# A ring of weight chunks in a mixture-of-experts loop: low parts written in place, eight slots instead of six, four high buffers instead of three

## The reference, cut to what matters

```python
def expert_block(args):
    tok, e = args
    xb = hf[tok]
    gu = xb @ w_gate_up[e] + b_gate_up[e]        # 1024 x 2048 per expert
    gate, up = jnp.split(gu, 2, axis=-1)
    gate = jnp.minimum(gate, SWIGLU_LIMIT)
    up = jnp.clip(up, -SWIGLU_LIMIT, SWIGLU_LIMIT)
    act = (up + 1.0) * gate * jax.nn.sigmoid(SWIGLU_ALPHA * gate)
    return act @ w_down[e] + b_down[e]           # 1024 x 1024 per expert
```

## Time and profile before

| | |
|---|---|
| median of 3 runs | 1774.97 us (1774.8 to 1775.13) |
| the profiled execution's own time | 1766.66 us |
| its span, first to last instruction | 1764.9 us |
| PE busy | 1698.8 us, 96% |
| DVE busy | 1381.7 us, 78% |
| ACT busy | 1200.8 us, 68% |
| POOL busy | 713.1 us, 40% |
| DMA moved | 504.64 MB, 286 GB/s over the span |

### The profile page before, as it was taken

How to read it: one execution, slowest core, us unless ns; L and a number is a source line. 1 busy time by engine, 2 the same in 40 slices (tenths; PEclk the granted TensorE clock), 3 DMA queues, 4 the chain that set the end, 5 groups by cost and what they waited for, 6 DMA issues and landing times.

```text
span 1764.9 us, 24895 instructions
## 1 busy us (share of the span) xinstructions
PE 1698.8 (96%) x8477; PEld 1346.8 (76%) x8477; DVE 1381.7 (78%) x1048; ACT 1200.8 (68%) x967; POOL 713.1 (40%) x344
## 2 busy tenths in 40 slices
PE   6999999999999999999999999999999999999998
PEld 5878889777888987767767767767767767767776
DVE  4666776755334389999999999999999999999984
ACT  5565555433223368788788788788788788788775
POOL 6124233550000072355465365365365365365110
PEclk9999999999999999999999999999999999999999
DMA  5443343433336469999999999999999999999951
GB/s 177 122 129 85 121 122 107 121 108 119 96 96 231 164 218 397 391 404 392 399 402 392 399 401 392 402 406 388 404 404 391 405 400 398 402 400 395 408 201 49
DMA packets 150865, 504.64 MB, mean 286 GB/s; under 512 B 12733, under 2 KB 73285, under 8 KB 117173
## 3 DMA queue, kind: packets, MB, share of 16 engines
q1 hardware_dynamic: 141652, 478.49, 70.0%
q0 software_dynamic: 9104, 25.28, 6.0%
q10 hardware_dynamic: 48, 0.07, 0.0%
HBM read 487.63 MB, written 20.28 MB: 288 GB/s over the span
## 4 chain that ended last, share of the span: by engine, by line
PE 68%; DVE 14%; issue 9%; ACT 6%; POOL 2%; DVEq 0%; ACTq 0%; POOLq 0%
PE gu_ps L2395 13%; DVE split_l L1928 9%; PE gu_ps L2147 8%; PE gu_ps L2149 8%; PE gu_ps L2148 8%; PE dn_ps L2453 7%; PE gu_ps L2399 7%; PE dn_ps L2459 3%; ACT split_h L1303 3%; PE gu_ps L2409 2%; PE dn_ps L2652 1%; PE gu_ps L2652 1%; PE et_ps L2381 1%; DVE up_sb L1915 1%; PE gu_ps L2169 1%
## 5 line engine op out<-in xcount | busy, mean ns | idle before, releaser
L1928 DVE TENSOR_TENSOR split_l<-ring,split_h 128x2048 fp32r<-128x2048 f32 x384 | 864.8, 2285 | 71.0 <-ACT split_h L1303 69.3
L1303 ACT ACTIVATE split_h<-ring 128x2048 fp32r<-128x2048 f32 x384 | 729.9, 1913 | 113.8 <-PE gu_ps L2399 62.7
L914 POOL COPY icur<-slots 96x1 int32 x30 | 282.8, 9428 | 412.3 <-PE et_ps L2381 410.1
L1536 DVE TENSOR_TENSOR w_lo<-w_raw,w_hi 128x2048 fp32r<-128x2048 f32 (+1 forms) x45 | 104.3, 2318 | 128.8 <-ACT w_hi L1035 122.6
L2409 PE MATMUL gu_ps<-split_l,xgT_h 128*128 128x512 f32 x480 | 139.6, 412 | 17.8 <-DVE split_l L1928 14.0
L2147 PE MATMUL gu_ps<-hT_h,w_hi 128*128 128x512 f32 x392 | 154.6, 394 | 0.6 <-DVE acc L1589 0.6
L2149 PE MATMUL gu_ps<-hT_h,w_lo 128*128 128x512 f32 x392 | 152.7, 390 | 0.0
L2148 PE MATMUL gu_ps<-hT_l,w_hi 128*128 128x512 f32 x392 | 152.6, 389 | 0.0
L2395 PE MATMUL gu_ps<-split_h,xgT_h 128*128 128x512 f32 x512 | 140.6, 396 | 0.9 <-DVE xgT_l L1934 0.9
L2399 PE MATMUL gu_ps<-split_l,xgT_h 128*128 128x512 f32 x512 | 137.2, 390 | 0.0
L2395 PE MATMUL gu_ps<-split_h,xgT_l 128*128 128x512 f32 x512 | 137.2, 390 | 0.0
(11 more groups left out here) (426 smaller groups left out, 3242.1 us busy)
## 6 DMA issues: line engine op xcount, KB each, us to landing
ring<-in_w_gate_up SPq DMA_DIRECT2D x256, 1024.0 KB, 8.0
ring<-in_w_down SPq DMA_DIRECT2D x128, 1024.0 KB, 9.2
w_raw<-in_w_in SPq DMA_DIRECT2D x28, 1024.0 KB, 5.9
arow<-acum_rows POOLq DMA_DIRECT2D x16, 512.0 KB, 6.5
w_raw<-in_w_ssd_out SPq DMA_DIRECT2D x8, 1024.0 KB, 5.4
w_raw<-in_w_in SPq DMA_DIRECT2D x9, 512.0 KB, 6.1
w_raw<-in_w_mix_out SPq DMA_DIRECT2D x4, 1024.0 KB, 7.9
wpg<-in_w_ple_gate SPq DMA_DIRECT2D x2, 2048.0 KB, 19.9
```

What stands on the lines that cost most here:

```text
L914: g.tensor_copy(icur[:, :], col).then_inc(idx_done, 1)
L1303: a.activation(split_h[s % SPLIT][:, :], ring[s % RING][:, :], ACT.Copy).then_inc(hi_done, 1)
L1536: v.tensor_tensor(w_lo[RAW_SLOT[n]][:, 0:size], w_raw[RAW_SLOT[n]][:, 0:size], w_hi[HI_SLOT[n]][:, 0:size].bitcast(F32), ALU.subtract).the ...
L1928: v.tensor_tensor(split_l[s % SPLIT][:, :], ring[s % RING][:, :], split_h[s % SPLIT][:, :].bitcast(F32), ALU.subtract).then_inc(lo_done, 1)
```

## The change

Low parts are written over the raw chunk in the ring slot (`ring_low` is the same memory as `ring`, in the fast matmul type), `split_l` goes, and its 24 KB become the fourth `split_h` and ring slots 6 and 7. A load now waits until PE has used the chunk eight before it. `high` waits for the chunk four before it. 12 chunks an expert are no multiple of 8 slots, so loops run over pairs of experts (24 chunks). In the seams, `gate` and `halves_out` now come behind `high` 10, `half_gate` behind `high` 11, `turned_high` and `turned_low` behind chunk 12 and chunk 16, `half_down_out` behind `high` 14, `half_y_out` and `y_out` behind `high` 15. The first loads of slots 6 and 7 wait for nothing. The diff, cut to its core (the same renaming of slots in the five matmul functions is left out):

```diff
-RING = 6
-SPLIT = 3
+RING = 8
+FIRST = 6
+SPLIT = 4
...
-        ring = [here(f"ring{i}", [P, 2 * DM], F32) for i in range(RING)]
+        ring_off = top[0]
+        ring = [here(f"ring{i}", [P, 2 * DM], F32) for i in range(FIRST)]
+        top[0] = ring_off
+        ring_low = [here(f"ring_low{i}", [P, 2 * DM], F32R) for i in range(FIRST)]
...
         split_h = [here(f"split_h{i}", [P, 2 * DM], F32R) for i in range(SPLIT)]
-        split_l = [here(f"split_l{i}", [P, 2 * DM], F32R) for i in range(SPLIT)]
+        ring_off = top[0]
+        ring += [here(f"ring{i}", [P, 2 * DM], F32) for i in range(FIRST, RING)]
+        top[0] = ring_off
+        ring_low += [here(f"ring_low{i}", [P, 2 * DM], F32R) for i in range(FIRST, RING)]
...
         def chunk_at(j, e, i):
-            return j * NE * CHUNKS + e * CHUNKS + UP + i
+            pair, off = in_pair(e)
+            return j * NE * CHUNKS + pair * (2 * CHUNKS) + off * CHUNKS + UP + i
+
+        def slot_of(e, i):
+            return (in_pair(e)[1] * CHUNKS + UP + i) % RING
...
             def gate_up(j, e, i, of, k, first=False):
-                slot = (UP + i) % RING
+                slot = slot_of(e, i)
                 if not first:
-                    sp.wait_ge(lo_done, chunk_at(j, e, i) + 1)
+                    sp.wait_ge(chunk_used, chunk_at(j, e, i) + CHUNKS - RING + 1)
...
-            for k in range(RING, UP):
-                gate_up(0, 0, k - UP, 0, k)
+            for k in range(FIRST, UP):
+                gate_up(0, 0, k - UP, 0, k, True)
...
             def high(j, e, i):
                 at, s = chunk_at(j, e, i), UP + i
-                act.wait_ge(e_loaded[s % RING], raw_loaded(j, e, i))
+                act.wait_ge(e_loaded[slot_of(e, i)], raw_loaded(j, e, i))
                 act.wait_ge(chunk_used, at + CHUNKS - SPLIT + 1)
...
                 def rest(e, more, rows_in, rows_act, folds=None):
-                    turned_high(t0 + 3 + e * 2, xgT_h, rows_in, 1.0 if more else 1.0 / ALPHA)
-                    for i in range(12, 14):
-                        high(j, e, i)
+                    n = number(e)
+                    high(j, e, 12)
+                    turned_high(t0 + 3 + n * 2, xgT_h, rows_in, 1.0 if more else 1.0 / ALPHA)
+                    high(j, e, 13)
+                    high(j, e, 14)
                     if folds is not None:
-                        half_down_out(e, e)
-                    high(j, e, 14)
+                        half_down_out(e, n)
+                    high(j, e, 15)
                     if folds is None:
-                        y_out(j, e, 11, n0 + e)
+                        y_out(j, e, 11, n0 + n)
                     else:
-                        half_y_out(e, folds)
-                    high(j, e, 15)
+                        half_y_out(n, folds)
                     if more:
-                        turned_high(t0 + 4 + e * 2, actT_h, rows_act, 1.0 / ALPHA)
-                        for i in range(16, 22):
+                        high(j, e, 16)
+                        turned_high(t0 + 4 + n * 2, actT_h, rows_act, 1.0 / ALPHA)
+                        for i in range(17, 22):
                             high(j, e, i)
 
                 def expert(e, more, rows_in=ROWS, folds=None):
-                    gate(j, e, UP - 1, n0 + e + 1)
                     high(j, e, 10)
+                    gate(j, e, UP - 1, n0 + number(e) + 1)
                     high(j, e, 11)
...
                 def half_expert(e, folds):
-                    halves_out(e, e + 1)
                     high(j, e, 10)
+                    halves_out(e, number(e) + 1)
+                    high(j, e, 11)
                     half_gate(folds)
-                    high(j, e, 11)
...
             def low(j, e, i):
                 dve.wait_ge(hi_done, at + 1)
-                v.tensor_tensor(split_l[s % SPLIT][:, :], ring[s % RING][:, :], split_h[s % SPLIT][:, :].bitcast(F32),
-                                ALU.subtract).then_inc(lo_done, 1)
+                v.tensor_tensor(ring_low[slot_of(e, i)][:, :], ring[slot_of(e, i)][:, :],
+                                split_h[s % SPLIT][:, :].bitcast(F32), ALU.subtract).then_inc(lo_done, 1)
...
                 def expert(e, more, half_next=False):
-                    up(ROWS, chunk_used, chunk_at(j, e, UP - 1) + CHUNKS + 1, n0 + e + 1)
                     low(j, e, 10)
+                    up(ROWS, chunk_used, chunk_at(j, e, UP - 1) + CHUNKS + 1, n0 + number(e) + 1)
                     low(j, e, 11)
```

More of the change, by code:

```diff
@@ L520, in program @@
         pen_done, last_idx = sem("pen_done"), sem("last_idx")
-        e_loaded = [sem(f"e_loaded{i}") for i in range(RING)]
+        e_loaded = [sem(f"e_loaded{i}") for i in range(FIRST)] + yT_loaded[0:RING - FIRST]
         hi_done, lo_done, et_hi = sem("hi_done"), sem("lo_done"), sem("et_hi")
@@ L729, in weights, with expert_loads @@
                     sp.wait_ge(order_done, 1)
-                with sp.Fori(1 if ahead else 0, NE - 1) as e:
-                    of, after = (position(sp, e), position(sp, e + 1)) if ahead else (e, e + 1)
-                    bias_parts(j * NE + e + 1, after)
+                def expert_loads(e):
+                    n = number(e)
+                    of, after = (position(sp, n), position(sp, n + 1)) if ahead else (n, n + 1)
+                    bias_parts(j * NE + n + 1, after)
                     for k in range(UP):
@@ L736, in weights @@
                         down(j, e, UP + r, of, r)
+                with sp.Fori(0, PAIRS) as i:
+                    for off in (1, 2) if ahead else (0, 1):
+                        expert_loads((i, off))
+                if not ahead:
+                    expert_loads(NE - 2)
                 of = position(sp, NE - 1) if ahead else NE - 1
@@ L748, in weights @@
                 alone(sp)
-            for k in range(RING):
+            for k in range(FIRST):
                 gate_up(0, 0, k - UP, 0, k, True)
@@ L1300, in high @@
                 at, s = chunk_at(j, e, i), UP + i
[L1301 removed]
+                act.wait_ge(e_loaded[slot_of(e, i)], raw_loaded(j, e, i))
                 act.wait_ge(chunk_used, at + CHUNKS - SPLIT + 1)
[L1303 removed]
+                a.activation(split_h[s % SPLIT][:, :], ring[slot_of(e, i)][:, :], ACT.Copy).then_inc(hi_done, 1)
             def gate(j, e, i, n):
@@ L1425, in one_pass @@
                     with act.Fori(0, PAIRS - 1) as i:
-                        expert(i * 2 + 2, True, HALF, i * 2 + 2)
-                        half_expert(i * 2 + 3, i * 2 + 3)
+                        expert((i, 2), True, HALF, i * 2 + 2)
+                        half_expert((i, 3), i * 2 + 3)
                     expert(NE - 2, False, folds=NE - 2)
                 else:
-                    with act.Fori(0, NE - 2) as e:
-                        expert(e, True)
+                    with act.Fori(0, PAIRS) as i:
+                        expert((i, 0), True)
+                        expert((i, 1), True)
                     expert(NE - 2, False)
@@ L2012, in one_pass @@
                     with dve.Fori(0, PAIRS - 1) as i:
-                        expert(i * 2 + 2, True, True)
-                        half_expert(i * 2 + 3, i * 2 + 3)
-                else:
-                    with dve.Fori(0, NE - 2) as e:
-                        expert(e, True)
+                        expert((i, 2), True, True)
+                        half_expert((i, 3), i * 2 + 3)
+                else:
+                    with dve.Fori(0, PAIRS) as i:
+                        expert((i, 0), True)
+                        expert((i, 1), True)
                 expert(NE - 2, False)
@@ L2403, in half_gate_up @@
             def half_gate_up(e, i, k):
-                at, s = chunk_at(0, e, i), (UP + i) % SPLIT
-                for part, ready, count in ((split_h, hi_done, at + 1), (split_l, lo_done, at + RING + 1)):
+                at, high_part, low_part = chunk_at(0, e, i), split_h[(UP + i) % SPLIT], ring_low[slot_of(e, i)]
+                for part, ready, count in ((high_part, hi_done, at + 1), (low_part, lo_done, at + RING + 1)):
                     pe.wait_ge(ready, count)
                     for b in range(4):
-                        o = t.matmul(gu_ps[:, b * 512:b * 512 + 512], xgT_h[:, k, :], part[s][:, b * 512:b * 512 + 512],
+                        o = t.matmul(gu_ps[:, b * 512:b * 512 + 512], xgT_h[:, k, :], part[:, b * 512:b * 512 + 512],
                                      start=False, stop=False)
@@ L2423, in half_down @@
             def half_down(e, r):
-                at, s = chunk_at(0, e, UP + r), (2 * UP + r) % SPLIT
-                for part, ready, count in ((split_h, hi_done, at + 1), (split_l, lo_done, at + RING + 1)):
+                at, high_part, low_part = chunk_at(0, e, UP + r), split_h[(2 * UP + r) % SPLIT], ring_low[slot_of(e, UP + r)]
+                for part, ready, count in ((high_part, hi_done, at + 1), (low_part, lo_done, at + RING + 1)):
```

(4 more changed lines are left out.)

75 lines of the change are left out of this document (42 added, 33 removed).

## The result

The changed kernel takes 1858.24 us (median of 4 runs, 1854.7 to 1860.93) where the kernel before took 1775.05 beside it: a ratio of 1.0467 (95% interval 1.0451 to 1.0484), 83 us slower. The forecast was 1759 with a range to 1785. It failed in its sign; the third rival named this place and 1859 us. The profiled execution is that of 1860.93 us, its span 1859.2.

The account below looks back on a forecast made before the run. Three high buffers were taken to bind, loads next at 64.8 us a pair: 15 x 1.0 + 0.8 = 15.8 us off 1775.0 gives 1759 us, range 1741 to 1785 (forecast's own range 1747 to 1770).

Parts of the forecast that it names:

- What bounds before: Expert loop: three high buffers limit DVE's lead, so PE waits 5.3 us a pair for low parts at half chunks.
- Part 1: Four high buffers: one chunk more lead cuts PE's wait from 5.3 to 2.6 us, the pair from 65.8 to 63.1.
- Part 2: Loads of a pair: bounds 63.2 on average and 65.8 us, 64.8 taken; loads late next, gain 1.0 us a pair.
- Part 3: Ring of eight slots released by PE: taken as 0, bounds -0.5 to +0.9 us a pair.
- Part 4: Low parts written in place by DVE: same instruction and size, taken as 0, at most 0.4 us a pair.
- Part 5: Seams, start and end: reordered instructions and start 0, the stretch behind the last pair -0.8 us.
- rival 3: POOL gets no turn in DVE's longer runs, so the index copy and gather come late: up to 1859 us; chance 0.20.
- end case: Worst case of rival 3: index copy 16.8 us later, PE loses up to 8.7 us a pair, 84 us net, 1859 us.
- the rule: Shared port pair held for one instruction's length: POOL's copy would wait some 2.2 us, the change cost nothing.
- Rival 1: The lead counts in full: gathers cost the ring less, pair 63.1 us, gain 40 us, 1735 us; chance 0.13.
- Rival 2: DMA engines full already: gain at most 0.3 us a pair, 1770 to 1775 us; chance 0.22.

Follow-up runs that it names:

- e9: Kernel before the change with each w_down load halved (a sixth of the loads' bytes less), engine work as before: 1774.83 us, ratio 0.9997.
- e10: e5 with each w_down load halved, engine work as before: 1745.3 us, ratio 0.9832 to the kernel before.
- e13: e5 with POOL's copies of the scatter's index and the next weight moved ahead of the wait for the transposes: ratio 1.0058 to the kernel before.
- e5: Changed kernel, with DVE waiting in the seam ahead of a half stretch until POOL's index copy is done: 1774.3 us, ratio 1.0041 to the kernel before.
- e1: Changed kernel without the fourth high buffer and with the old seams; in-place low parts and eight slots kept: 1771.97 us, ratio 1.0029 to the kernel before.
- e2: Changed kernel with POOL's index copy moved ahead of its wait for the transposes: 1780.95 us, ratio 1.0074 to the kernel before.
- e12: Kernel before the change with POOL's index copy moved ahead of its wait for the transposes: 1778.35 us, ratio 1.0014.
- e15: e2 with the scatter's index and next weight copied early too, and DVE waiting until the gather is issued: ratio 1.0116 to the kernel before.
- e14: e2 with the scatter's index and next weight copied early too, no pause of DVE: ratio 1.0048 to the kernel before.
- e11: Changed kernel with each w_down load halved, engine work and index copy as they were: 1841.69 us, ratio 1.0371 to the kernel before.
- e6: Changed kernel with each low part made by two DVE subtractions of half the size: 1883.46 us, ratio 1.0664 to the kernel before.
- e8: e2 with halves_out back ahead of high 10 and DVE pausing until the gather is issued: 1781.47 us, ratio 1.0082 to the kernel before.

## Why the prediction was wrong

**What bounds before.** Right. The three buffers did, not the loads: e9 has a sixth fewer bytes and the same 65.8 us.

**Part 1.** Right in mechanism and nearly in size. PEld's waits for low parts fell from 5.3 to 1.4 us a pair, further than the 2.6 forecast, and with loads and POOL out of the way a pair takes 63.6 us (e10), where 63.1 was worked out.

**Part 2.** The order was right (the loads are late next), the size wrong. The pair with whole loads is 66.0 to 66.2 us (e13, e5), not 64.8. I took a value below the upper bound of 65.8 although the queues' shares summed to 101%; the upper bound itself was too low. The gain of 1.0 us a pair was none. That is 15 us of the miss of 99.

**Part 3.** Taken as 0. In the pairs that holds (e1, 65.8 us); behind the last pair all kernels with eight slots lose 5 us, by a stall of ACT that nothing in the traces explains. The bounds did not cover an end of the program.

**Part 4.** Right: the subtraction takes 2285 ns in place, in 384 instructions, as in the row of before at 2.29.

**Part 5 and the sum.** Here the forecast failed. The sum had no term for POOL; its whole lateness stood in rival 3, at 0.20 and "most of it near the small end". In place of nothing it was 6.6 us of wait of PE and 2.2 of lower clock in the pair shown; less what the lead gained that is 5.9 us a pair, 82 in all. The rival's chain of reasons was right: DVE's runs without a pause keep POOL out, the change makes them longer, and PE's slack of 4.8 to 8.1 us is used up (7.0 us of the delay went into it). Its end case gave 8.7 us of wait and 84 us, against 8.8 of wait and clock together and 83 us. That the totals meet so closely is partly luck: the end case delayed the copy by 16.8 us, where copy and issue together came 13.6 us later, and it had neither the clock nor the 5 us at the end. Two things made me hold the rival for small. I asked how much later the copy would end, and it was only 2.2 us longer (12.54 against 10.32). That the issue behind it would meet the next run of subtractions, 14.05 us instead of 2.70, was not asked, though the earlier trace rows had a sign of it: the issue starts at 1028.20, just behind the gap in which the copy ended and inside a subtraction, and ends at 1030.90. And "if loads bind, DVE must pause somewhere" let one term hide the other: the loads would have bound at 66, but by then PE had already stopped for the rows, and the loads never got late.

I let the rule weigh against the row as well. The Trainium skill, SBUF — State Buffer, section SBUF: two separate sides, has the loser of the shared port pair wait for one whole instruction. The traces here go against that as a bound: POOL waited through runs of four, six and twelve. The same section warns of DMAs issued by GpSimd, whose descriptors can't be written while VectorE runs an instruction in a two-port mode. The 14.05 us look like such a wait, and I had not read it onto this gather. The section Who interferes with whom excludes tensor_tensor from the effect on descriptors, by inference, and has it contend with GpSimd's reads. In the changed kernel, e2, e5 and e12 the issue takes 9 to 14 us beside little but tensor_tensor; whether it waits to read its indices or to write its descriptors no run here tells.

**Rivals.** Rival 1 (1735) is what e10 comes near with light loads. Rival 2 (nothing gained, 1770 to 1775) is what is left when POOL's lateness is repaired: 1.0041 in e5, 7 us, of which the stall at the end is some 5. Rival 3 is what happened.

A version that beats the kernel before with whole loads was not found. The fourth buffer with its seams buys nothing as long as the loads need 66 us a pair.

## What to carry to other kernels

When a change makes VectorE run without gaps, list every instruction of GpSimd that overlaps such a run, the issues of indirect DMAs as well as the copies, and price each at the whole run rather than at one instruction. Add the times in series, then compare them with the slack of the engine that needs the result. If they don't fit, a semaphore wait of VectorE where GpSimd has to act can be cheap: in e5 one took 76 us back. A wait for the longer step isn't sure to be: e15 lost 13 us against e14, for a cause that is open. And before widening a buffer, run the old kernel and the new with fewer bytes loaded, to see which of them the loads hold. A larger wait can hide the answer: e11 still stood at 1841.69 us, and only e10, with POOL's lateness repaired, showed the loads.

## What the runs showed of the hardware

- GpSimd's copy of 96 numbers takes 0.18 us at the least (in the changed kernel) and up to 27.51 us (e6) beside VectorE subtractions with both inputs in SBUF; the issue of an indirect DMA 1.0 us and up to 15.8 (e8). Idle gaps of VectorE of 0.19 to 0.44 us were enough to let it in (the copy of dcur in e5 ends at 1046.09, in the one of 0.19 us; the index copy of the kernel before in the one of 0.44); more boundaries without gaps were not (e6).
- Of VectorE instructions that read PSUM some let it in and some don't: the one of 0.68 us at 1051.87 of the changed kernel did not with a subtraction right behind it, and did in e5, where the subtraction had to wait. The difference between 1061.27 (changed kernel) and 1061.60 (e6) is open.
- After a wait of PE of 6.6 us the matmuls ran at the clock's lower level, 1.2 GHz, for some 4.5 us (granted clock 0.52 from 1085.30 to 1088.30), and the mean of the 14 us around such a wait is 0.76. In e13 a wait of 2.78 us had the same after it (granted clock 0.50 from 856.20 to 860.00).
